# The last layer norm split in two passes: every row while the last three jobs run, then the rows of those jobs once more

## The reference, cut to what matters

```
moe_params = (w_router[l], b_router[l], w_gate[l], b_gate[l], w_up[l], b_up[l], w_down[l], b_down[l])
x = layer_norm(DEEPNORM_ALPHA * x + g2 * moe_ffn(modulate(x, sh2, sc2), *moe_params), ln2_g[l], ln2_b[l])

def layer_norm(x, g, b):
    mu = xf.mean(-1, keepdims=True)
    var = jnp.square(xf - mu).mean(-1, keepdims=True)
    return (xf - mu) * lax.rsqrt(var + LN_EPS) * g + b
```

## Time and profile before

| | us |
|---|---|
| median of 3 runs | 2350.78 |
| profiled execution | 2349.14 |
| its span | 2347.4 |
| PE busy | 2188.0 (93%) |
| DVE busy | 1018.9 (43%) |
| ACT busy | 464.3 (20%) |
| POOL busy | 445.0 (19%) |

### The profile page before, as it was taken

The page is one execution under the profiler, slowest core; times in us unless marked ns, Lnnn a source line. Parts: engine busy times, 40 slices in busy tenths (PEclk is TensorE's granted clock), DMA queues, the critical chain, the costliest instruction groups (busy, mean ns, idle before and its releaser), DMA issues.

```text
span 2347.4 us, 33576 instructions
## 1 busy us (share of the span) xinstructions
PE 2188.0 (93%) x9959; PEld 1019.5 (43%) x9960; DVE 1018.9 (43%) x1587; ACT 464.3 (20%) x624; POOL 445.0 (19%) x417
## 2 busy tenths in 40 slices
PE   6889999779958999999998999999999999999995
PEld 3444444464544444443443344444443444444442
DVE  2665743556675233444334242423253333222235
ACT  2333443331210111111111111111111111111113
POOL 0000100001321122222222232312113222122110
PEclk9999999889969999999999999999999999999997
DMA  9121310012253676889489999647899558897644
...
DMA packets 169065, 510.55 MB, mean 217 GB/s; under 512 B 16530, under 2 KB 51098, under 8 KB 167866
## 3 DMA queue, kind: packets, MB, share of 16 engines
...
## 4 chain that ended last, share of the span: by engine, by line
PE 84%; DVE 7%; DMA 3%; SPq 2%; issue 2%; ACT 1%; DVEq 0%; POOL 0%; POOLq 0%
PE psall L591 27%; PE psall L619 14%; PE psall L595 10%; PE psall L776 9%; PE psall L623 4%; PE psall L600 4%; PE psall L764 3%; DMA arena<-in_w_down_dram 2%; PE psall L887 2%; PE psall L881 2%; PE psall L743 1%; PE psall L660 1%; PE psall L628 1%; SPq L431 1%; DVE arena L1438 1%
## 5 line engine op out<-in xcount | busy, mean ns | idle before, releaser
L591 PE MATMUL psall<-arena 128*128 128x512 f32 x1472 | 646.9, 598 | 27.9 <-issue 22.6
L591 PEld LDWEIGHTS psall<-arena 128*128 128x128 f32 x1472 | 279.9, 192 | 373.3 <-issue 373.3
L619 PE MATMUL psall<-arena 128*128 128x512 f32 x736 | 322.5, 597 | 5.5 <-DVE arena L1807 4.0
L595 PE MATMUL psall<-arena 128*64 128x512 f32 x1152 | 259.3, 602 | 9.9 <-DMA arena<-in_w_up_dram 4.2
L1633 DVE STREAM_TRANSPOSE arena<-arena 128x1024 f32<-128x1024 f32 x49 | 61.0, 1245 | 456.0 <-PE psall L591 276.4
L776 PE MATMUL psall<-arena 128*128 128x512 f32 (+1 forms) x560 | 229.2, 567 | 0.0
L619 PEld LDWEIGHTS psall<-arena 128*128 128x128 f32 x736 | 139.5, 191 | 182.9 <-issue 182.9
L1232 ACT COPY arena<-psall 128x512 f32<-128x512 f32 x49 | 28.7, 586 | 790.1 <-PE psall L660 790.1
L1807 DVE COPY arena<-psall 128x512 f32<-128x512 f32 x49 | 33.9, 691 | 324.4 <-PE psall L660 324.0
L1235 ACT ACTIVATE arena<-arena 128x1024 f32<-128x1024 f32 x49 | 51.8, 1057 | 584.3 <-DVE arena L1641 584.3
L1908 POOL DMA_INDIRECT arena<-h_rows,lruw x144 | 147.0, 1021 | 82.6 <-POOL lruw L1901 39.4
...
## 6 DMA issues: line engine op xcount, KB each, us to landing
arena<-in_w_gate_dram SPq DMA_DIRECT2D x128, 1024.0 KB, 5.7
arena<-in_w_up_dram SPq DMA_DIRECT2D x128, 1024.0 KB, 8.4
arena<-in_w_down_dram SPq DMA_DIRECT2D x128, 1024.0 KB, 8.5
...
arena<-in_x_dram SPq DMA_DIRECT2D x16, 512.0 KB, 6.8
arena<-in_w_in_dram SPq DMA_DIRECT2D x16, 512.0 KB, 4.0
...
```

The lines of the kernel that those rows point to most:

```text
L591: mm = pe.matmul(ps[2 * g + s], xT[:, k, :], w[:, s * BANK:(s + 1) * BANK], start=(k == 0), stop=(k == KD - 1))
L595: mm = pe.matmul(ps[2 * g][HT * j:HT * j + HT, :], xT[:, k, 0:HT], w[:, j * BANK:(j + 1) * BANK], start=(k == 0), stop=(k == KD - 1), skip ...
L619: mm = pe.matmul(ps[6 + s], aT[:, k, :], w[:, s * BANK:(s + 1) * BANK], start=(k == 0), stop=(k == KD - 1))
```

## The change

- SP no longer loads anything at the end; it only stores the eight tiles of `fin` as they come.
- PE no longer adds C's rows (`sum_rows` is gone), and DVE no longer builds `last_is`.
- `fin` moves to an area that is free during the jobs, `ln2r` to rows of `adarow`.
- ACT, in the iteration in which B is at its activation, issues from its own queue the eight loads of `fin` (after J's scatter has landed) and behind them the two of `ln2r`, and then forms the statistics of all eight tiles (`row_total` to `row_std`).
- DVE normalises tiles 0 to 3 in that iteration behind `weigh` of A, and tiles 4 to 7 in the next, behind its copy of B's `aT` and ahead of `swiglu` of C.
- POOL holds A's scatter back until all eight tiles are loaded. In the next iteration it gathers A's rows of the stream (`late_rows(0)`), once all of C's gate and up product is done; ACT forms their statistics behind C's sigmoid (`late_stats(0)`), and DVE finishes them behind its copy of C's `aT`.
- C is not scattered. `weigh_last` leaves its contribution in `gb`. Behind its loops POOL waits for B's scatter, gathers the rows of B and of C, and then writes the rows of A, B and C to the output by three indirect stores, each waiting for the one before.
- Every iteration reads more of the table: POOL two more rows where a job is at its scatter, DVE and ACT one more row.

The diff, cut to its core:

```diff
-        fin = reg(0, NT, D)
-        ln2r = reg(8192, 2, D)
-
-        EARLY = 4
-        last_is = reg(O_X1 + 4096, EARLY, P)
-        last_tok = lw[:, 620:621]
+        fin = reg(O_X1, NT, D)
+        ln2r = adarow[:, 0:2]
+        late = reg(0, 3, D)
+        tok_before = lw[:, 1024 + 8 * JOBS - 1:1024 + 8 * JOBS + JW - 1].bitcast(I32)
...
-            njobs = sp.value_load(tab[0:1, J_NJ:J_NJ + 1], min_val=SEQ * TOPK // P, max_val=MAXJ)
-            others = sp.value_load(tab[0:1, ds(njobs * NC + J_STORED, 1)], min_val=16, max_val=16 * P)
-            sp.wait_ge(gu_used, njobs * GUP)
-            settle(sp)
-            for i, v in enumerate((ln2_g, ln2_b)):
-                sp.dma_start(ln2r[:, i], v.partition_broadcast(P).rearrange("p a n -> p (a n)")).then_inc(d_ln2, 16)
-            sp.wait_ge(y_stored, others)
-            settle(sp)
-            for t in range(EARLY):
-                sp.dma_start(fin[:, t], acc_dram[t * P:(t + 1) * P, :]).then_inc(d_fin[t], 16)
-
-            sp.wait_ge(y_stored, njobs * 16)
-            settle(sp)
-            for t in range(EARLY, NT):
-                sp.dma_start(fin[:, t], acc_dram[t * P:(t + 1) * P, :]).then_inc(d_fin[t], 16)
...
-            njobs = pe.value_load(tab[0:1, J_NJ:J_NJ + 1], min_val=SEQ * TOPK // P, max_val=MAXJ)
-            weighed = pe.snap(njobs + 2, min_val=3, max_val=MAXJ + 2)
-            for T in range(EARLY):
-                pe.wait_ge(d_fin[T], 16)
-                sum_rows(T, ident[:, :], fin[:, T], True)
-                if T == 0:
-                    pe.wait_ge(y_dve, weighed)
-                    settle(pe)
-                sum_rows(T, last_is[:, T, :], yb, False).then_inc(half_mm, 1)
...
+            def row_total(T):
+                act.wait_ge(d_fin[T], 16)
+                act.activation(fin[:, T], fin[:, T], ACT.Copy, accum_out=ln_sum[:, T:T + 1]).then_inc(row_mid, 1)
+
+            def row_mean(T):
+                act.wait_ge(row_mid, 2 * T + 1)
+                act.activation(ln_neg[:, T:T + 1], ln_sum[:, T:T + 1], ACT.Copy, scale=-1.0 / D).then_inc(row_mid, 1)
...
+            def late_stats(i):
+                n = 2 * NT + 2 * i
+                act.activation(late[:, i], late[:, i], ACT.Copy, accum_out=late_sum[:, i:i + 1]).then_inc(row_mid, 1)
+                act.wait_ge(row_mid, n + 1)
+                act.activation(late_neg[:, i:i + 1], late_sum[:, i:i + 1], ACT.Copy, scale=-1.0 / D).then_inc(row_mid, 1)
+                act.wait_ge(row_mid, n + 2)
+                act.activation(sg, late[:, i], ACT.Square, bias=late_neg[:, i:i + 1], accum_out=late_sq[:, i:i + 1]).then_inc(row_sq, 1)
+                act.wait_ge(row_sq, NT + i + 1)
+                act.activation(late_std[:, i:i + 1], late_sq[:, i:i + 1], ACT.Sqrt, scale=1.0 / D, bias=eps_ln[:, :]).then_inc(std_ready, 1)
+
+            def load_stream(u):
+                stored = act.value_load(tab[0:1, ds(u * NC + J_STORED, 1)], min_val=16, max_val=16 * P)
+                act.wait_ge(y_stored, stored)
+                settle(act)
+                for t in range(NT):
+                    act.dma_start(fin[:, t], acc_dram[t * P:(t + 1) * P, :]).then_inc(d_fin[t], 16)
+                spread = act.value_load(tab[0:1, ds(u * NC + (2 * NC + J_ORD), 1)], min_val=16, max_val=16 * NE)
+                act.wait_ge(bias_spread, spread)
+                settle(act)
+                for i, v in enumerate((ln2_g, ln2_b)):
+                    act.dma_start(ln2r[:, i], v.partition_broadcast(P).rearrange("p a n -> p (a n)")).then_inc(d_ln2, 16)
+
...
+                            with act.If(typ_of(act, typ_n) > 0):
+                                with act.If(typ_of(act, typ_m) < 1):
+                                    load_stream(u)
+                                    row_total(0)
+                                    row_mean(0)
+                                    act.wait_ge(act_ready, u + 2)
+                                    for T in range(NT):
+                                        if T + 1 < NT:
+                                            row_total(T + 1)
+                                        row_squares(T)
+                                        if T + 1 < NT:
+                                            row_mean(T + 1)
+                                        row_std(T)
+                                act.nop()
+                            with act.Else():
+                                act.wait_ge(act_ready, u + 2)
+                                settle(act)
+                                act.wait_ge(late_in, 16)
+                                late_stats(0)
+                            act.nop()
...
+            act.wait_ge(late_in, 48)
+            late_stats(1)
             act.wait_ge(var_ready, NT + 1)
+            act.activation(late_std[:, 2:3], mv[:, 1:2], ACT.Sqrt, bias=eps_ln[:, :]).then_inc(std_ready, 1)
...
+            def weigh_last(u, order_):
+                link(dve.tensor_copy(wcol, row_w[:, 0, ds(u, 1)]))
+                dve.wait_ge(dn_used, u * DNP + DNP)
+                dve.wait_ge(bdn_spread, order_)
+                link(dve.tensor_tensor(gb, psY, ebias[:, 2], ALU.add))
+                link(dve.scalar_tensor_tensor(out=gb, in0=gb, scalar=wcol, in1=adarow[:, 3], op0=ALU.mult, op1=ALU.mult))
+
+            def normalise(T):
+                dve.wait_ge(row_sq, T + 1)
+                dve.scalar_tensor_tensor(out=fin[:, T], in0=fin[:, T], scalar=ln_neg[:, T:T + 1],
+                                         in1=ln2r[:, 0], op0=ALU.add, op1=ALU.mult).then_inc(ln2_scaled, 1)
+                dve.wait_ge(std_ready, NT + T + 1)
+                link(dve.reciprocal(ln_r[:, T:T + 1], ln_std[:, T:T + 1]))
+                dve.wait_ge(ln2_scaled, T + 1)
+                dve.scalar_tensor_tensor(out=fin[:, T], in0=fin[:, T], scalar=ln_r[:, T:T + 1], in1=ln2r[:, 1],
+                                         op0=ALU.mult, op1=ALU.add).then_inc(fin_ready, 1)
+
+            def finish(i, neg, op):
...
+                        job_row(dve, [typ_n, ord_n], u + 2)
+                        job_row(dve, [typ_m], u + 3)
                         with dve.If(tp > 0):
                             dve.wait_ge(act_turned, u + 1)
                             dve.tensor_copy(aT[:, 4:8].rearrange("p k n -> p (k n)"), ps[5]).then_inc(aT_dve, 1)
-                        job_row(dve, [typ_n, ord_n], u + 2)
+                            with dve.If(typ_of(dve, typ_c) > 0):
+                                with dve.If(typ_of(dve, typ_n) < 1):
+                                    ch.n = chained + NT // 2
+                                    for T in range(NT // 2, NT):
+                                        normalise(T)
+                                dve.nop()
+                            with dve.Else():
+                                ch.n = chained + NT
+                                dve.wait_ge(row_sq, NT + 1)
+                                finish(0, late_neg[:, 0:1], ALU.add)
+                            dve.nop()
...
-                            with dve.If(typ_of(dve, typ_c) < 1):
-                                link(dve.tensor_copy(last_tok, tok_f[:, 0, ds(u, 1)]))
-                                for T in range(EARLY):
-                                    link(dve.tensor_scalar(last_is[:, T, :], slots, float(P * T), last_tok, ALU.add, ALU.is_equal))
-                            by_kind(dve, tp, lambda kind: weigh(u, kind, orderp))
+                            with dve.If(typ_of(dve, typ_c) > 0):
+                                by_kind(dve, tp, lambda kind: weigh(u, kind, orderp))
+                                with dve.If(typ_of(dve, typ_n) > 0):
+                                    with dve.If(typ_of(dve, typ_m) < 1):
+                                        dve.wait_ge(d_ln2, 32)
+                                        ch.n = chained
+                                        for T in range(NT // 2):
+                                            normalise(T)
+                                    dve.nop()
+                                dve.nop()
+                            with dve.Else():
+                                ch.n = chained + NT + 1
+                                weigh_last(u, orderp)
...
+            dve.wait_ge(row_sq, NT + 2)
+            finish(1, late_neg[:, 1:2], ALU.add)
+            dve.wait_ge(late_in, 48)
+            link(dve.tensor_tensor(late[:, 2], late[:, 2], gb, ALU.add))
+            for q in range(2):
+                link(dve.bn_stats(st[:, 6 * q:6 * q + 6], late[:, 2, q * BANK:(q + 1) * BANK]))
             link(dve.bn_aggr(mv, st))
             dve.nop().then_inc(var_ready, 1)
+            finish(2, mv[:, 0:1], ALU.subtract)
...
-                            pool.wait_ge(y_dve, u + 2)
-                            settle(pool)
                             tc = pool.value_load(tab[0:1, ds(u * NC + (NC + J_TYP), 1)], min_val=0, max_val=4)
-                            with pool.If(tc < 1):
```

(36 more changed lines are left out.)

104 lines of the change are left out of this document (41 added, 63 removed).

## The result

The change makes the kernel slower. The median of four runs is 2363.8 us (2360.17 to 2366.09) against 2350.2 us for four runs of before (2347.08 to 2353.74), ratio 1.0054, 95% interval [1.0042, 1.0067], which is 9.9 to 15.7 us. Forecast were 2364.8 us (2349 to 2370).

What follows compares the result with a forecast made beforehand. PE bounds the kernel until 2285 us; some 33 us then lie behind its last product, 20.7 of them DVE's passes. The terms ended the span at 2361.4 against 2347.4, 14.0 us more: 2364.8 us, range 2349 to 2370.

Steps and rivals of the forecast that it cites:

- Part 1: ACT's queue and DVE: `ln2r` lands last, at 2272.5, after 9.4 MB of loads, delaying `swiglu` of C by 11.1 us.
- Rival 2: Gain and bias rows land before DVE reaches them: delay 0.2 us, everything behind 10.9 us earlier, 2353.9 us; chance 18%.
- Part 2: ACT's statistics of A's rows delay its copy of C's `aT`: 2.5 us more on PE's path, costing nothing.
- Part 3: The tail: after B's scatter, POOL gathers from 2332.7, DVE's last pass ends at 2349.4, the store lands at 2354.8.
- 18.4, so 2330.4: POOL after B's scatter lands at 2312.0: row reads, branches and leaving the loops take 18.4 us, to 2330.4.
- leaves as before in 14.9 us: POOL's way out of its loops takes 14.9 us, as it did in the kernel before.
- DVE out of its loops 1.3 + 8.7 + 1.5 later: DVE's way out of its loops after PE's last down product ends at about 2336, 4 us ahead of 2340.7.
- rival 3: Rows early, DRAIN costing nothing, POOL's way out hidden: DVE leaving its loops sets the end, 2342.5 us; chance 9%.
- Part 4: End of program: POOL's DRAIN of 6.36 us, hidden before, now follows the last landing and ends at 2361.2.
- In the loop: Added table reads on POOL and DVE fall into existing waits: taken as 0, range 0 to 5 us.
- 1: Rival: POOL's DRAIN does not wait when a DMA has just landed, or overlaps it: 2358.4 us; chance 15%.
- 4: Rival: the longer loop bodies cost 3 us beside the forecast: 2368 us; chance 6%.

Runs made afterwards that it cites:

- x1: The changed kernel with ACT issuing the gain and bias rows ahead of the eight tiles instead of behind them: 2358.6 us, ratio 1.0029.
- x9: The changed kernel with DVE's passes of tiles 4 to 7 moved from ahead of `swiglu` of C to behind its copy of C's `aT`: 2357.32 us.
- x3: The changed kernel with the gathers of B's and C's rows moved into POOL's last loop iteration: 2364.16 us, ratio 1.0052.
- x2: The kernel before, with POOL made to wait behind its loops until SP's last output stores have landed: 2358.78 us, 6.8 us over its before.
- x4: The kernel before, with only the change's added table reads, unused: 2352.71 us against 2352.01, ratio 1.0007.
- x8_all: x7, with tiles 4 to 7 as in x9 and ACT's statistics of A's rows behind its copy of C's `aT`: 2342.89 us, ratio 0.9961.
- x7: x1 and x3 together, DVE's last passes in its loop, B's finished before `weigh_last`, SP instead of POOL awaiting the last stores: 2345.93 us.

## Why the prediction was right

**Part 1 was right, and shown by x1 and x9.** Less the 5.1 us ahead of S, the first pass of tile 0 starts at 2272.6 (forecast 2272.5), the copy of B's `aT` at 2285.7 (2285.0) and `swiglu` of C at 2296.7 (2296.1). The estimate that all 9.4 MB share 389 GB/s and that the last in the queue lands last met the row to 0.1 us, and not by luck: from 2253.5 to 2277.5 the DMA engines of after moved 390 GB/s. (The 1.0 us that the sum puts between the first issue and the first bytes has no row of its own.) Rival 2, early rows, is refuted: DVE waited for `in_ln_b_dram`. What the prediction did not see is that the order alone does not mend it: with the gain and bias rows first, the tiles and so ACT's statistics come late in their place, and 3.6 of the 11.7 us stay.

**Part 2 had the mechanism right and the size too large.** ACT's copy of C's `aT` (end 2313.84) comes 6.3 us behind DVE's last pass of C's activation (2307.56); forecast were 7.5. PE waits for ACT, not DVE. Before, PE's down product began 5.2 us behind the same pass (2295.89 less 2290.71), in after 6.3, so PE's path got 1.2 us longer by it and not 2.5. It cost nothing, as forecast, but with less room than forecast: this path was ready only 0.9 to 1.5 us ahead of POOL's (below).

**Part 3 had the mechanism right, with some terms mis-sized.** Less 5.1 us: B's scatter at 2308.3 (forecast 2308.1), the gathers at 2330.6 and 2332.0 (2332.7 and 2334.0), DVE's pass for B at 2339.2 (2340.7), its last pass ending at 2348.0 (2349.4). First, "18.4, so 2330.4" and two reads behind it: the rows show 19.8 us from the end of B's scatter to the first gather, where the sum had 24.6 from its start with 3.9 for the landing; after has 22.3 from start to start. The term that was too large is "leaves as before in 14.9 us": from the read that ends the iteration (L2055, at 2321.4) to the first read behind the loops (L2066, at 2333.7) it was 12.2. The way is the same, two empty iterations of 3.9 us and three outer tests of 1.2; but before, five of its table reads were slow. Instructions of the lines, first of before, then of after:

```profile
L1971 POOLq TENSOR_LOAD <-tab x2: 289/616/943, 2318.9 to 2323.9; - x2
L1978 POOLq TENSOR_LOAD <-tab x2: 293/534/774, 2320.3 to 2324.7; - x2
L1961 POOLq TENSOR_LOAD <-tab x3: 633/642/934, 2327.0 to 2330.3; - x3
```

```profile
L2055 POOLq TENSOR_LOAD <-tab x3: 288/289/289, 2321.4 to 2329.2; - x3
L2008 POOLq TENSOR_LOAD <-tab x3: 292/294/298, 2330.4 to 2332.8; - x3
```

The excess of the five over 0.29 us adds up to 2.5 us, which is the difference. Second, "DVE out of its loops 1.3 + 8.7 + 1.5 later" is 10.2 us from the start of the last weigh pass, and x3 shows 11.6 (0.6 of it again one slow table read, 1.11 us, which took 0.54 in after). That pass starts at 2326.1 less the shift, so this path was ready at 2337.8, not 2336, against 2339.2 for the other. The slack was 1.5 us by that and 0.9 by x3, not 4.7. Third, the store: 3.3 us to landing, not 4.5; the gathers took 3.9 in the median, as taken, but the second, for which ACT waits, took 4.5 from its issue (2337.14 to 2341.65). In rival 3, the terms 8.3 and 5.4 from 2325 give 2338.7 and not 2339.1, which changes nothing.

The Trainium skill, page "DMA: Bandwidth & Descriptors", section "Anatomy of one DMA — SWDGE (gpsimd) path", gives 3.2 us for 512 KB, an estimate worked out from its fit. The stores of these runs, 3.3 us, agree with it; the gathers, 3.9 in the median, are longer.

**Part 4 was right.** The DRAIN follows the last landing and takes 6.8 us (forecast 6.4). x2 shows by itself what POOL's being last costs: 6.8 us of the timed runs, with a DRAIN of 6.36. The diff does not show this term.

**In the loop, 0 was probably too low.** The end moved 11.9 us behind S, the ratio says 12.7. The excess, the timed difference to before less the one behind S, can be had for all kernels: it is 0.8, 3.4, 1.9, 1.7, 1.6, 2.6, 2.5, 2.4, 3.5 and 3.6 us for the ten with the longer loop bodies, in the table's order with x2 left out, and -0.6 us for x2, which has none. Each is uncertain by some 2 to 3 us, since it takes the time behind S from a single profile, and some share their runs of before; but all ten have one sign, and their mean is 2.4 us. So I read some 2 us for the added reads and the branches beside them, inside the range of 0 to 5. It is not shown by a run of its own: x4, which has the reads alone, has an interval that includes 0. Where in the loops they are spent is open. The tail was 2.1 us cheaper than forecast (11.9 against 14.0), and the loop, taken as 0, gave a part of it back (0.8 us in after's own runs): that the total came out nearer than its parts is luck.

**The rivals.** 1 is refuted by x2 and by after itself, 2 by the wait of 12.71 us, 3 with them; of 4, about 2 of the 3 us may be real. What the change is after was sound: the layer norm of most rows can be hidden, which x8_all shows with 11.6 us behind S. It was lost to three things outside the arithmetic: a place in a DMA queue with passes ahead of `swiglu` (11.7 us), the ways out of the loops (about 10), and POOL's DRAIN (6.8), of which x7 got back 2.5 by letting it run beside the last landing.
